# A two-block transformer kernel on one core: the last tiles before two inner norms by halves of the tokens, and the slabs behind each norm split early into memory that is no longer read

## The chip, the core and the metric

The kernel runs on one core of one Trainium2 chip. A core has TensorE (PE, with its weight loads listed as PEld), VectorE (DVE), ScalarE (ACT), GpSimd (POOL) and SyncE (SP), which here only starts transfers. Each engine works through its own list of instructions in order and waits at semaphores for the others. The metric is the device time of one execution in microseconds (us); lower is better.

## What is computed

Two transformer blocks, one behind the other, on 512 tokens of 1024 features, in float32. What matters here is cut out of them:

```python
# first block
mod = silu(c) @ w_ada + b_ada                  # six vectors: sh1, sc1, g1, sh2, sc2, g2
...
mix = concatenate([att, pool], -1) @ w_out
x = x + g1 * mix
h2 = rmsnorm(x, norm2_g) * (1.0 + sc2) + sh2   # "norm 1" below
x = x + g2 * conv_gated_ffn(h2, w_up, conv_w, conv_b, w_down)
# second block
h = rmsnorm_2(x, g_pre_mix) * (1.0 + sc1) + sh1   # "norm 2" below
proj = h @ w_in            # qa ka va qb kb vb, qi (heads i0..i3), ki, wi, two gates
...
def rmsnorm(x, g): return x * rsqrt(mean(x * x, -1) + EPS) * g
```

A norm needs the sum over all 1024 features, so it can't start for a token before the last tile of the product ahead of it is added to `x` for that token.

## The kernel before

The features lie on the 128 partitions, the tokens along the free axis: a *tile* m (0 to 7) is 128 features by 512 tokens, and one bank of PSUM holds one. Each float32 operand is split into a high and a low part (`HH`/`HL`, `WH`/`WL`), and a product is three matmuls per 128 input features: high by high, high by low, low by high. A tile of eight input tiles is so 24 matmuls, one of six input tiles 18.

Weights come as *slabs* of 256 columns (two tiles). SP loads slab i into `RAW[i % 2]` once slab i-2 is split; ACT copies it to `WH[i % 2]` (line 994) once PE has spent slab i-2, and POOL subtracts into `WL[i % 2]` (line 1916). Slabs 5 to 8 are `("out", 0..3)`, 9 and 10 `("gate", 0)` and `("val", 0)`, 39 to 42 `("down", 2, 0..3)`, 43 `ki` (which also holds `wi`), 44 `i01`, 45 `vb0`, 46 `i23`. Between the slabs SP loads the chunks of the modulation matrix (`ada`, 512 KB each, into `ZF`): chunk n+2 once VectorE has taken chunk n (lines 1495 and 1498). A plan (`ada_plan`) fixes at which point of the program each chunk is taken: `("1", s)` is step s of the first attention, `("2", p)` the slab p of the output product, and `sums` says where PE turns the finished vector (line 563).

Around norm `st` (1 or 2) the order was: for each tile m, VectorE adds the product to `x` (lines 1618 and 1664), ACT squares it (998) and multiplies it by its gain (1151), VectorE adds up the squares (1458). Then `norm_two` sums over the partitions with a matrix of ones, ACT takes logarithm and exponential (1013, 1015), VectorE refines the root in four instructions (1442 to 1450, `newton`), multiplies the eight tiles (1478), ACT adds the shift into `HH` (1022), VectorE forms `HL` (1483), and PE's `first_slab` starts. `first_slab` goes over the high parts of its two tiles first and then over the low ones.

Behind norm 2 come the products `ki`, `wi`, `i0` and then steps s of the indexer: scores of head pair c at even steps, a `piece` (half a product) of `i1`, `vb0`, `vb1`, `i2`, `i3`, `bq0`, `bk0` at the steps of `T_I`. `i` products leave out the first 128 tokens (384 columns). Before the scores of step 0, VectorE, POOL and ACT rotate and split `i0`.

Of the kernel before, what the change touches and what calls it, by code (L numbers as in the profile page):

```python
# [13 lines left out]
T = 512  # L14
D = 1024
# [170 lines left out]


# [132 lines left out]
def ada_plan():  # L320
# [22 lines left out]
class Kernel:  # L343


    def __init__(self, nc, ctx, a):
# [95 lines left out]
    def wbuf(self, of, i):  # L442
        nk, nn, _ = self.slabs[self.names[i]]
        return of[:, i % 2, 0:nk * nn].rearrange("p (k n) -> p k n", k=nk)
# [12 lines left out]
T_I = {"i1": 0, "vb0": 2, "vb1": 4, "i2": 6, "i3": 11, "bq0": 16, "bk0": 18}  # L457
# [25 lines left out]
def pe_program(pe, k):  # L483
# [18 lines left out]
    def slab(name, j=7):  # L502
# [3 lines left out]
        return k.wbuf(k.WH, i), k.wbuf(k.WL, i)  # L506
# [19 lines left out]
    def first_slab(name, keys, st):  # L526
# [13 lines left out]
        spend(name, keys[1])  # L540

# [169 lines left out]
    for m in range(4, 8):  # L711
        mix(m, 0, 8)
        if m % 2:
            for p in (m // 2 - 2, m // 2):
                for j in k.sums["2", p]:
                    ada_sum(j)
    norm_two(1)


    def up1(i):  # L720
        c0, n = UP1[i]
        for p in range(c0, c0 + n, 2):
            for g in ("gate", "val"):
                if (g, p) == ("gate", 0):
                    first_slab((g, p), ((g, 0), (g, 1)), 1)
                else:
# [6 lines left out]
    def down(what, i, n):  # L733
# [3 lines left out]
        for p in range(4):  # L737
# [3 lines left out]
            for j in k.sums.get((what, i, p), ()):  # L741
                ada_sum(j)

    up1(0), up1(1), down("down", 0, 8), up1(2), down("down", 1, 8), down("down", 2, 6)
    norm_two(2)


    first_slab("ki", ("ki", "wi"), 2)
    B.deal(main=range(4), s=range(4, 8))

# [13 lines left out]
    piece("i0", 0)  # L764
    piece("i0", 1)
# [5 lines left out]
    for s in range(STEPS_I):  # L771
# [12 lines left out]
        for x, t0 in T_I.items():  # L784
            if 0 <= s - t0 < 2:
# [186 lines left out]
def act_program(act, k):  # L972
# [44 lines left out]
    def shifted(st, shift):  # L1017

        for j in range(8):
            act.wait_ge(v_h["prod", st, j])  # L1020
            act.wait_ge(v_ada["mod", shift])
            e.activation(k.HH[:, j, :], k.slot(j), ACT.Identity, bias=k.MOD[:, shift, j:j + 1]).then_inc(*hh.hit((st, j)))
# [124 lines left out]
    def gain(st, j, ready):  # L1147
        act.wait_ge(ready)
        act.wait_ge(v_ada["gain", st])
        row = {1: 0, 2: 0}[st]  # L1150
        e.activation(k.slot(j), k.XT[:, j, :], ACT.Copy, scale=k.GS[:, row, j:j + 1]).then_inc(*sq.hit(("gain", st, j)))

    for m in range(8):
        if m == 0:
            for q in range(4):
                weights(q)
        elif m in (4, 6):
            weights()
        square_two(1, m, k.XT[:, m, :], v_post["x1", m])
        gain(1, m, v_post["x1", m])  # L1160
    root(("norm", 1), norm_full[1, 7], 1.0 / D, k.RB[:, :])
# [1055 lines left out]
```

## Time and profile before

| | |
|---|---|
| Time, three runs | 1565.91, 1566.36 and 1566.45 us (median 1566.36) |
| The profiled execution | 1566.11 us |
| Its span, first to last instruction | 1564.1 us |
| PE busy | 1411.2 us (90%) |
| VectorE, ScalarE, GpSimd busy | 827.2, 624.4, 705.3 us (53%, 40%, 45%) |
| Chain that ended last, by engine | PE 69%, DVE 15%, ACT 7%, POOL 5%, DMA 2% |
| Mean granted TensorE clock | 0.956 of full speed |

PE is the engine whose work bounds the kernel, so time is lost mainly where PE is idle, and where its clock is at the lower level after that. A row of a timeline gives start, length, engine, line, operation, output and inputs, shape and count, and in brackets the idle time of the engine ahead of it and what ended it.

### The profile page before, as it was taken

What the parts mean: (1) busy time and instruction counts of PE and PEld (TensorE: products, weight loads), DVE (VectorE), ACT (ScalarE), POOL (GpSimd) and SP (SyncE); (2) the same over time, 40 slices, a digit from 0 to 9 for tenths busy, and PEclk for the clock granted to TensorE, in tenths of its full rate; (3) what the DMA queues carried; (4) which work ended last, traced back from release to release, by engine and by line L of the source; (5) the groups of instructions that cost most, each with busy time, mean ns of one, the idle gap of its engine ahead of it and who ended that gap; (6) DMA issues with size and microseconds to landing.
All of it is one profiled execution on the core that took longest, in us unless ns stands there. A gap on an engine that the chain in (4) does not pass through costs nothing.

```text
span 1564.1 us, 16757 instructions
## 1 busy us (share of the span) xinstructions
PE 1411.2 (90%) x6633; PEld 1140.2 (73%) x6633; DVE 827.2 (53%) x1210; ACT 624.4 (40%) x1018; POOL 705.3 (45%) x328
## 2 busy tenths in 40 slices
PE   4679897899999999858999999999878999999995
PEld 2558775688878888657787777788755888888884
DVE  5686525766673563536789975542248321312125
ACT  3345533434341432424466654454334431413231
POOL 1155533455654464234233453335544664646442
PEclk8799998999999999979999999999989999999997
DMA  8424216265656564311122221112221333232311
GB/s 289 139 69 129 82 53 213 70 200 177 198 168 211 175 188 143 101 54 54 54 72 64 77 59 54 54 55 81 81 81 37 98 108 99 90 108 81 108 54 54
DMA packets 143870, 167.49 MB, mean 107 GB/s; under 512 B 14256, under 2 KB 129584, under 8 KB 143792
## 3 DMA queue, kind: packets, MB, share of 16 engines
q1 hardware_dynamic: 143792, 166.42, 34.4%
q8 instruction: 52, 0.85, 0.2%
q14 instruction: 26, 0.21, 0.0%
HBM read 164.31 MB, written 2.10 MB: 106 GB/s over the span
## 4 chain that ended last, share of the span: by engine, by line
PE 69%; DVE 15%; ACT 7%; POOL 5%; DMA 2%; issue 2%; SPq 0%; ACTq 0%; DVEq 0%
PE B L495 66%; POOL WL L1916 4%; ACT WH L994 2%; DVE ZF L1498 1%; DVE SC L1798 1%; DVE SC L1565 1%; DVE ZF L1769 1%; DVE ZF L1854 1%; PE B L563 1%; DVE XT L1856 1%; PE B L661 1%; DVE SC L1447 1%; PE B L839 1%; DVE M L1767 1%; DVE SC L1657 1%
## 5 line engine op out<-in xcount | busy, mean ns | idle before, releaser
L1916 POOL TENSOR_TENSOR WL<-RAW,WH 128x512 fp32r<-128x512 f32 (+2 forms) x175 | 519.4, 2974 | 577.9 <-ACT WH L994 577.8
L495 PE MATMUL B<-HH,WH 128*128 128x512 f32 (+1 forms) x1088 | 442.7, 407 | 47.2 <-POOL WL L1916 23.5
L495 PE MATMUL B<-HH,WL 128*128 128x512 f32 (+1 forms) x1088 | 432.6, 398 | 0.0
L495 PE MATMUL B<-HL,WH 128*128 128x512 f32 (+1 forms) x1088 | 417.8, 393 | 0.0
L495 PE MATMUL B<-ZR,WH 128*128 128x512 f32 x1184 | 367.2, 391 | 6.4 <-POOL ZR L1923 5.0
L994 ACT ACTIVATE WH<-RAW 128x512 fp32r<-128x512 f32 (+2 forms) x175 | 211.7, 1225 | 215.8 <-PE B L495 160.0
L495 PEld LDWEIGHTS B<-HH,WH 128*128 128x128 f32 x1088 | 211.3, 194 | 100.2 <-issue 49.1
L495 PEld LDWEIGHTS B<-ZR,WH 128*128 128x128 f32 x1184 | 223.2, 189 | 53.9 <-POOL ZR L1923 5.4
L495 PEld LDWEIGHTS B<-HH,WL 128*128 128x128 f32 x1088 | 211.0, 194 | 44.3
L495 PEld LDWEIGHTS B<-HL,WH 128*128 128x128 f32 x1088 | 208.5, 192 | 39.0 <-issue 0.5
L495 PE MATMUL B<-ZR,WL 128*128 128x512 f32 x592 | 231.1, 390 | 0.0
L495 PE MATMUL B<-ZR 128*128 128x256 f32 (+4 forms) x904 | 126.7, 328 | 29.6 <-POOL ZR L1923 11.0
L1923 POOL TENSOR_TENSOR ZR<-SC,ZR 128x512 fp32r<-128x512 f32 (+1 forms) x72 | 95.2, 1323 | 117.4 <-ACT ZR L1390 52.8
L495 PEld LDWEIGHTS B<-ZR 128*128 128x128 f32 (+1 forms) x904 | 98.6, 190 | 58.2 <-issue 22.8
L495 PEld LDWEIGHTS B<-ZR,WL 128*128 128x128 f32 x592 | 111.8, 189 | 23.5
L1874 DVE TENSOR_TENSOR SC<-SC 128x512 f32<-128x512 f32 x32 | 56.5, 1766 | 109.8 <-ACT SC L1385 109.8
L1498 DVE SCALAR_TENSOR_TENSOR ZF<-ZF,CA 128x1024 f32<-128x1024 f32 x68 | 96.3, 1417 | 8.1 <-DMA ZF<-in_w_ada 4.9
L1639 DVE SCALAR_TENSOR_TENSOR SC<-B,VT,SC 128x511 f32<-128x511 f32 x44 | 32.9, 747 | 81.4 <-ACT SC L1171 81.4
L1885 DVE TENSOR_TENSOR ZF<-B,ZF 128x512 f32<-128x512 f32 x24 | 16.6, 692 | 101.1 <-PE B L495 101.1
L1321 ACT ACTIVATE ZR<-B 128x128 fp32r<-128x128 f32 (+3 forms) x64 | 28.0, 437 | 101.5 <-PE B L839 101.3
L1458 DVE TENSOR_TENSOR SC<-SC 128x512 f32<-128x512 f32 x24 | 31.7, 1319 | 54.0 <-ACT SC L998 54.0
L1786 DVE TENSOR_TENSOR ZR<-B,ZR 128x128 fp32r<-128x128 f32 (+3 forms) x64 | 31.3, 488 | 51.6 <-ACT ZR L1321 51.3
(188 smaller groups left out, 1343.5 us busy)
## 6 DMA issues: line engine op xcount, KB each, us to landing
ZF<-in_w_ada SPq DMA_DIRECT2D x86, 512.0 KB, 4.3
RAW<-in_w_ff SPq DMA_DIRECT2D x32, 1024.0 KB, 5.3
RAW<-in_w_up SPq DMA_DIRECT2D x22, 1024.0 KB, 8.3
RAW<-in_w_in SPq DMA_DIRECT2D x16, 1024.0 KB, 5.2
RAW<-in_w_in SPq DMA_DIRECT2D x19, 512.0 KB, 5.2
RAW<-in_w_down SPq DMA_DIRECT2D x8, 1024.0 KB, 7.6
G<-in_w_ada SPq DMA_DIRECT2D x10, 512.0 KB, 8.4
RAW<-in_w_out SPq DMA_DIRECT2D x4, 1024.0 KB, 5.0
```

The lines of the kernel that those rows point to most:

```text
L495: return e.matmul(out, l, r, start=start, stop=stop)
L563: t = e.transpose(b[:, 128 * i:128 * i + 128], k.ACC[j % 2][:, 512 * half + 128 * i:512 * half + 128 * i + 128], k.IDN)
L994: e.activation(k.WH[:, i % 2, at], k.RAW[:, i % 2, at], ACT.Copy).then_inc(*w.hit((i, q)))
L1321: e.activation(k.PT2[:, u % 2, 0, KEYS[blk], 128 * (blk % 2):128 * (blk % 2) + 128], B["t2", u][:, 0:128 * (blk + 1)].rearrange("p (j n) - ...
L1458: e.tensor_tensor(k.slot(8), k.slot(8), k.slot(9), ALU.add).then_inc(*acc.hit((st, j)))
L1498: e.scalar_tensor_tensor(out=dst, in0=src, scalar=c, in1=dst, op0=ALU.mult, op1=ALU.add).then_inc(*ada.hit((j, kt)))
L1639: e.scalar_tensor_tensor(out=s[:, 1:T], in0=b[:, 0:T - 1], scalar=k.VT[:, 128 + c:129 + c], in1=s[:, 1:T], op0=ALU.mult, op1=ALU.add).then ...
L1786: e.tensor_tensor(lo, B["t2", u][:, 0:128 * (blk + 1)].rearrange("p (j n) -> p j n", j=blk + 1), hi.bitcast(F32), ALU.subtract).then_inc(* ...
L1874: e.tensor_tensor(k.xg(ch), k.xg(ch), k.xg(ch), ALU.mult).then_inc(*ffn.hit(("sq", ch)))
L1885: e.tensor_tensor(y, b[:, :], y, ALU.add).then_inc(*post.hit(("yadd", i, m)))
L1916: e.tensor_tensor(k.WL[:, i % 2, at], k.RAW[:, i % 2, at], k.WH[:, i % 2, at].bitcast(F32), ALU.subtract).then_inc(*w.hit((i, 3 if q is No ...
L1923: e.tensor_tensor(dst, src, hi.bitcast(F32), ALU.subtract).then_inc(*sig.hit(key))
```

## The change

The tiles 4 to 7 ahead of norms 1 and 2 are computed in two passes, first for tokens 0 to 255 and then for tokens 256 to 511 (`TILES`, `last_tiles`). The norm of the first half is made while PE works on the second pass (`norm_half`, called after four input tiles of tile 4 of the second pass). The matmuls behind the norm are ordered so that four output tiles of two slabs are done by halves (`first_slabs`): `gate 0, gate 1, val 0, val 1` behind norm 1 and `ki, wi, i0, i1` behind norm 2. `i0` and `i1` are now computed for all 512 tokens. The two slabs that these read are split into parts of `ZR` that nothing reads any more (`away`), so they don't wait for a slab to be spent. Slabs around the norms are split in quarters of 512 columns (`quarters`). The plan moves the eight chunks of vector 3 out of the output product and into steps 31 to 38 of the attention, and SP queues the chunks two slabs later. `vb0` moves from steps 2 and 3 to ahead of step 0, and four small copies on ACT move behind the steps of the indexer.

```diff
-        many = {"1": p % 2 == 0 and p < 32, "2": (3, 3, 2, 0)[p % 4], "gate": 2, "val": 2, "down": 2 - point[1]}[g]
+        many = {"1": p % 2 == 0 if p < 31 else 1, "2": 0, "gate": 2, "val": 2, "down": 2 - point[1]}[g]
...
+        self.away = {("gate", 0): 8192, ("val", 0): 12288, "ki": 8192, "i01": 12288}
...
-T_I = {"i1": 0, "vb0": 2, "vb1": 4, "i2": 6, "i3": 11, "bq0": 16, "bk0": 18}
+T_I = {"i1": -2, "vb0": 2, "vb1": 4, "i2": 6, "i3": 11, "bq0": 16, "bk0": 18}
...
+    def first_slabs(names, keys, st, norm):
...
+        high(0, 0)
+        norm()
+        high(0, 1), high(0, 2), high(0, 3)
+        low(0, 0), low(0, 1), low(0, 2), low(0, 3)
+        high(1, 0), high(1, 1), low(1, 0), low(1, 1)
+        spend(names[0], keys[1])
+        high(1, 2), high(1, 3), low(1, 2), low(1, 3)
...
+    def norm_half(st, half):
+
+        b, at = B.take(pe, "main", ("norm", st, half)), HALF[half]
+        pe.wait_ge(acc[st, 6, half])
+        mm(b[:, at], ONES[:, :], k.slot(8)[:, at], True, False)
+        pe.wait_ge(sq[st, 7, half])
+        mm(b[:, at], ONES[:, :], k.slot(9)[:, at], False, True).then_inc(*norm_full.hit((st, 7, half)))
+
+    def last_tiles(tile, norm):
+
+        for half in range(2):
+            for m in range(4, 8):
+                if (m, half) == (4, 1):
+                    tile(m, half, 0, 4)
+                    norm()
+                    tile(m, half, 4, None)
+                else:
+                    tile(m, half, 0, None)
...
+    def norm_by_halves(st, shift, ready, after, between):
+
+
+        for m, half in TILES:
+            between(m, half)
+            square_half(st, m, half, k.XT[:, m, :], ready[(*after, m, half)])
+            if half == 1:
+                shifted(st, shift, 0, (2 * m - 8, 2 * m - 7))
+            if m == 7:
+                at = HALF[half]
+                root(("norm", st, half), norm_full[st, 7, half], 1.0 / D, k.RB[:, at], at)
+            gain(st, m, half)
+        between(8, None)
+        shifted(st, shift, 1)
...
+    def between1(m, half):
+        if (m, half) in ((0, None), (4, 0), (6, 0), (7, 0)):
+            quarters()
...
+    def between2(m, half):
+        if (m, half) in ((2, None), (4, 0), (6, 0)):
+            quarters()
+        if (m, half) in ((4, 1), (5, 1)):
+            quarters(2 * m - 8, 2 * m - 6)
...
+        for m, half in TILES:
+            tile(m, half)
+            add_half(st, m, half)
+            if (m, half) == (7, 0):
+                root(0)
+            if half == 1 and m < 7:
+                products(st, 0, range((0, 3, 6)[m - 4], (3, 6, 8)[m - 4]))
+        low(st, shift, 0, range(5))
+        root(1)
+        low(st, shift, 0, range(5, 8))
+        products(st, 1)
+        low(st, shift, 1)
...
-        point = ("2", k.names[i][1]) if k.names[i][0] == "out" else k.names[i]
-        for n in k.chunks.get(point, ()):
+        for n in k.chunks.get(k.names[i - 2], ()):
             ada(n + 2)
```

SP's queue from the load of `("out", 2)` on, before (`ZF` is a chunk of the modulation matrix, `RAW` a slab, of which `out` takes three transfers):

```order
L2095 DMA RAW<-in_w_out 64x4x256 [waits pool_w]
L2095 DMA RAW<-in_w_out 64x4x256
L2095 DMA RAW<-in_w_out 128x4x256
L2095 DMA ZF<-in_w_ada 128x1024 [waits dve_ada] x3
L2095 DMA RAW<-in_w_out 64x4x256 [waits pool_w]
L2095 DMA RAW<-in_w_out 64x4x256
L2095 DMA RAW<-in_w_out 128x4x256
L2095 DMA ZF<-in_w_ada 128x1024 [waits dve_ada] x3
L2095 DMA RAW<-in_w_up 128x8x256 [waits pool_w]
L2095 DMA ZF<-in_w_ada 128x1024 [waits dve_ada] x2
```

and in the changed kernel, where the first row stands in the steps of the attention:

```order
L2264 DMA ZF<-in_w_ada 128x1024 [waits dve_ada] x8
L2264 DMA RAW<-in_w_out 64x4x256 [waits pool_w]
L2264 DMA RAW<-in_w_out 64x4x256
L2264 DMA RAW<-in_w_out 128x4x256
L2264 DMA RAW<-in_w_out 64x4x256 [waits pool_w]
L2264 DMA RAW<-in_w_out 64x4x256
L2264 DMA RAW<-in_w_out 128x4x256
L2264 DMA RAW<-in_w_up 128x8x256 [waits pool_w] x5
L2264 DMA ZF<-in_w_ada 128x1024 [waits dve_ada] x2
```

Eight chunks stand ahead of `("out", 2)` that stood behind it and behind `("out", 3)`; between the last slabs of the output product there is none.

ScalarE's list from the split of slab 8 to the last square of the output product, before:

```order
L994 ACTIVATE WH<-RAW 128x2048 [waits pe_proj,in_w0]
L998 ACTIVATE SC<-XT 128x512 [waits dve_post,dve_acc]
L1151 ACTIVATE SC<-XT,GS 128x512
L998 ACTIVATE SC<-XT 128x512 [waits dve_post,dve_acc]
L1151 ACTIVATE SC<-XT,GS 128x512
L994 ACTIVATE WH<-RAW 128x2048 [waits pe_proj,in_w1]
L998 ACTIVATE SC<-XT 128x512 [waits dve_post,dve_acc]
L1151 ACTIVATE SC<-XT,GS 128x512
```

and now, for the first pass (line 1091 is the copy of a slab, 1118 the square, 1277 the gain):

```order
L1118 ACTIVATE SC<-XT 128x256 [waits dve_acc,dve_post]
L1277 ACTIVATE SC<-XT,GS 128x256
L1091 ACTIVATE ZR<-RAW 128x512 [waits pe_weigh,in_w1]
L1091 ACTIVATE ZR<-RAW 128x512 x3
L1118 ACTIVATE SC<-XT 128x256 [waits dve_acc,dve_post]
L1277 ACTIVATE SC<-XT,GS 128x256
L1091 ACTIVATE ZR<-RAW 128x512 [waits in_w0]
L1091 ACTIVATE ZR<-RAW 128x512 x3
L1118 ACTIVATE SC<-XT 128x256 [waits dve_acc,dve_post]
L1123 ACTIVATE RB<-B,EPSC 128x256 [waits pe_norm]
```

The copies of slabs 9 and 10 now stand ahead of the squares of tiles 6 and 7 of the first pass, and the second of them waits for a transfer.

## Rows read from the trace of the kernel before

**Rows 1.** Stretches: busy of PE, PEld, DVE, ACT, POOL; granted clock; DMA share, GB/s

```profile
226.00:316.00 90.00, 73.32 (x299) 58.28 (x297) 54.20 (x61) 36.17 (x47) 35.15 (x11) 0.89 0.43 132
316.00:586.00 270.00, 268.17 (x1200) 220.75 (x1200) 166.73 (x173) 98.01 (x101) 149.07 (x44) 1.00 0.60 187
632.00:730.00 98.00, 72.72 (x323) 58.65 (x321) 50.62 (x60) 34.05 (x52) 36.25 (x14) 0.90 0.27 75
```

**Rows 2.** Chain that ended last, 236 to 262 us: start, length, what

```profile
237.90 3.55 DMA ZF<-in_w_ada
...
241.47 1.29 DVE ZF L1498
...
244.46 6.31 DMA RAW<-in_w_out
...
252.78 5.09 POOL WL L1916
```

**Rows 3.** Timeline of PE around norm 1

```profile
258.00 0.77 PE L495 MATMUL B<-HH,WH 128*128 128x512 f32 x1 [10.67 <-POOL WL L1916]
...
271.83 1.03 PE L563 MATMUL B<-CST,ZF 128*128 128x128 f32 x8
...
279.87 0.77 PE L495 MATMUL B<-HH,WH 128*128 128x512 f32 x1 [5.19 <-ACT HH L1022]
...
289.42 3.79 PE L495 MATMUL B<-HL,WH 128*128 128x512 f32 x16
```

**Rows 4.** Timeline of PE around norm 2 and up to the indexer

```profile
653.92 1.10 PE L495 MATMUL B<-SC,ONES 128*128 128x512 f32 x2 [1.16 <-DVE SC L1458]
...
661.52 0.76 PE L495 MATMUL B<-HH,WH 128*128 128x512 f32 x1 [5.19 <-ACT HH L1022]
...
682.91 0.66 PE L495 MATMUL B<-HH,WH 128*128 128x384 f32 x1 [7.73 <-POOL WL L1916]
...
689.18 0.49 PE L769 MATMUL B<-CST,SC 128*128 128x128 f32 x3
...
697.67 1.01 PE L495 MATMUL B<-ZR 64*128 64x256 f32 x6 [8.01 <-POOL ZR L1923]
```

**Rows 5.** Timeline of PE: first and last of six short waits for a slab

```profile
316.07 0.47 PE L495 MATMUL B<-HH,WH 128*128 128x512 f32 x1 [0.89 <-POOL WL L1916]
...
586.28 0.70 PE L495 MATMUL B<-ZR,WH 128*128 128x512 f32 x2 [0.28 <-POOL WL L1916]
```

**Rows 6.** Timeline of PE: matmuls of 256 columns, and the row behind them

```profile
146.59 3.12 PE L495 MATMUL B<-ZR 128*128 128x256 f32 x24
...
149.55 0.40 PE L495 MATMUL B<-HH,WH 128*128 128x512 f32 x1
```

**Rows 7.** Weight loads grouped by line and form: busy, mean ns, idle before

```profile
L495 PEld LDWEIGHTS B<-HH,WH 128*128 128x128 f32 x1088 | 211.3, 194 | 100.2 <-issue 49.1 <-POOL HL L1923 3.6 <-POOL WL L1916 2.2
```

**Rows 8.** Timeline of SP

```profile
203.06 0.33 SPq L2095 DMA_DIRECT2D ZF<-in_w_ada  x1
...
243.15 1.91 SPq L2095 DMA_DIRECT2D RAW<-in_w_out  x3
```

**Rows 9.** Timeline of VectorE and GpSimd where they meet

```profile
235.00 1.18 DVE L1458 TENSOR_TENSOR SC<-SC 128x512 f32<-128x512 f32 x1 [3.19 <-ACT SC L998]
...
231.82 5.50 POOL L1916 TENSOR_TENSOR WL<-RAW,WH 128x512 fp32r<-128x512 f32 x4 [8.26 <-ACT WH L994]
...
691.14 4.76 DVE L1565 TENSOR_TENSOR SC<-SC 128x384 f32<-128x384 f32 x1 [0.65 <-POOL SC L1928]
...
690.99 4.50 POOL L1916 TENSOR_TENSOR WL<-RAW,WH 128x2048 fp32r<-128x2048 f32 x1
```

**Rows 10.** Timeline of VectorE and ScalarE: the products, a short form, small copies

```profile
278.28 4.91 DVE L1478 TENSOR_TENSOR SC<-SC,RB 128x512 f32<-128x512 f32 x8
...
699.11 0.35 DVE L1746 TENSOR_SCALAR ZF<-SC,WI 128x256 f32<-128x256 f32 x1 [3.20 <-ACT SC L1278]
...
665.97 0.71 ACT L1233 ACTIVATE ZR<-CST 128x256 fp32r<-128x256 f32 x2
```

More of the change, by code:

```diff
@@ L184, with tokens, before @@
 UP1 = [(0, 8), (8, 8), (16, 6)]
+HALF = [slice(0, 256), slice(256, 512)]
+TILES = [(m, None) for m in range(4)] + [(m, h) for h in range(2) for m in range(4, 8)]
+def tokens(h):
+    return slice(0, 512) if h is None else HALF[h]
+def before(m, h):
+    return (m - 1, None) if m < 5 else (m - 1, h)
 ORDER2 = ("bq1 bk1 ga0 ga1 ga2 ga3 bq2 bk2 vb2 vb3 ga4 ga5 bq3 bk3 ga6 ga7 aq0 ak0 va0 va1 aq1 ak1 aq2 ak2 va2 va3 "
@@ L710, in pe_program, with out_tile @@
     mix(3, 4, 8)
[L711 to L717, printed above, removed]
+    for j in k.sums["2", 0]:
+        ada_sum(j)
+    def out_tile(m, half, j0, j1):
+        proj(("mix", m, half), ("out", m // 2), 128 * (m % 2), mix_xs, j0, j1, half=half)
+        if half and m % 2 and j1 is None:
+            spend(("out", m // 2), ("mix", m, half))
+    last_tiles(out_tile, lambda: norm_half(1, 0))
     def up1(i):
@@ L736, in down @@
             pe.wait_ge(g_ffn[what, i, j])
-        for p in range(4):
+        last = (what, i) == ("down", 2)
+        for p in range(2 if last else 4):
             proj((what, i, 2 * p), (what, i, p), 0, xs)
@@ L742, in down, with tile @@
                 ada_sum(j)
+        if last:
+            def tile(m, half, j0, j1):
+                proj((what, i, m, half), (what, i, m // 2), 128 * (m % 2), xs, j0, j1, half=half)
+                if half and m % 2 and j1 is None:
+                    spend((what, i, m // 2), (what, i, m, half))
+            last_tiles(tile, lambda: norm_half(2, 0))
     up1(0), up1(1), down("down", 0, 8), up1(2), down("down", 1, 8), down("down", 2, 6)
-    norm_two(2)
-    first_slab("ki", ("ki", "wi"), 2)
-    B.deal(main=range(4), s=range(4, 8))
+    first_slabs(("ki", "i01"), ("ki", "wi", "i0", "i1"), 2, lambda: norm_half(2, 1))
+    mine = [B.of[x] for x in ("ki", "wi", "i0", "i1")]
+    B.deal(main=mine, s=[b for b in range(8) if b not in mine])
     def piece(x, ph):
@@ L784, in pe_program @@
         for x, t0 in T_I.items():
-            if 0 <= s - t0 < 2:
+            if 0 <= s - t0 < 2 and x not in ("i1", "vb0"):
                 piece(x, s - t0)
@@ L1144, in act_program, with gain @@
             weights(SPLIT1[s])
-    def gain(st, j, ready):
-        act.wait_ge(ready)
+    def gain(st, j, half):
         act.wait_ge(v_ada["gain", st])
[L1150 to L1161, printed above, removed]
-    e.preload_act_table_set(SILU)
-    shifted(1, 3)
+        at = tokens(half)
+        e.activation(k.slot(j)[:, at], k.XT[:, j, at], ACT.Copy, scale=k.GS[:, 0, j:j + 1]).then_inc(
+            *sq.hit(("gain", st, j, half)))
+    def between1(m, half):
+        if (m, half) in ((0, None), (4, 0), (6, 0), (7, 0)):
+            quarters()
+        if m == 8:
+            e.preload_act_table_set(SILU)
+    norm_by_halves(1, 3, v_post, ("x1",), between1)
     def tap(g, ch, n):
@@ L1281, in act_program @@
             task(x, s, t0)
+    for dst, src in ((k.IDR, k.IDN), (k.CAR, k.CAUS)):
+        e.activation(dst, src, ACT.Copy)
+    for half in range(2):
+        e.activation(k.PT2[:, half, :, 3, 0:128], k.CST[:, 0:256].rearrange("p (a n) -> p a n", a=2), ACT.Copy, scale=0.0)
     act.wait_ge(score_full["i", 23])
@@ L1864, in dve_program @@
         e.tensor_scalar(k.slot(m), k.XT[:, m, :], k.GS[:, 2, m:m + 1], None, ALU.mult).then_inc(*hl.hit(("gain", 4, m)))
-    normed(4)
+    newton(("norm", 4), 1.0 / D, k.RB[:, :], k.slot(8), k.slot(9))
+    dve.wait_ge(root_["y", ("norm", 4)])
+    for j in range(8):
+        product(4, j)
     low(4, 9)
@@ L1991, in pool_program @@
             low(k.HL[:, g, :], k.MEAN[g], k.HH[:, g, :], a_mix["pool", g], mix, ("pool", g))
[L1994 to L1997 removed]
+    for i in range(5):
+        quarters()
     def up1(i):
@@ L2012, in pool_program @@
     up1(2)
-    for p in range(8):
+    for p in range(4):
         weights()
+    for p in range(4):
+        quarters()
     def task(x, s, t0):
```

218 lines of the change are left out of this document (135 added, 83 removed).

## The prediction, written before the changed kernel was run

> **What bounds the kernel now.** I read the busy shares first: PE is busy 90% of the span, so I looked for the stretches in which it is not. The view by stretches shows three kinds [rows 1]. In the feed-forward part (316 to 586 us) PE is busy 268.17 of 270 us at full clock; there is almost nothing to win. From 226 to 316 us it is busy 73.32 of 90, from 632 to 730 us 72.72 of 98, and in both the granted clock is 0.89 and 0.90, so busy time is lost too. These are the two norms. The waits of PE in them, read from its timeline, give the terms of the sum.
>
> At norm 1 PE stands twice [rows 3]: 10.67 us for a slab, and 5.19 us for the norm itself. After each it runs at the lower clock level: the 48 matmuls from 258.00 to 271.83 took 13.83 us where the pitch at the upper level, (3.79 - 0.39)/15 = 0.227 us [rows 3], makes 10.9; the 32 from 279.87 to 289.42 took 9.55 where it makes 7.3. So norm 1 costs 10.67 + 5.19 + 2.9 + 2.3 = 21.1 us. The chain says why the slab was late [rows 2]: SP could load it only after a modulation chunk had landed (3.55 us) and VectorE had taken it; then the slab took 6.31, and GpSimd 5.09 for its low part.
>
> At norm 2 the waits are 1.16, 5.19, 7.73 (slab `i01`, split behind the rotation of `ki`) and 8.01 (the rotated `i0`, ahead of the first scores) [rows 4], together 22.1; two smaller ones of about 1.0 lie beside them. The lower clock: behind 661.52 as at norm 1, 2.3; from 682.91 to 689.18 24 matmuls of 384 columns took 6.27 us where 24 x 0.227 x 384/512 = 4.1 is due, 2.2; behind 697.67 some 1.5 (estimated as a share of these, from six score matmuls that took 1.01). Sum 22.1 + 1.0 + 6.0 = 29.1 us.
>
> **The change part by part.**
>
> *The waits removed.* With two passes, PE has the second pass (at norm 1 four tiles of 3 us) in front of it while the first half's norm is made, and behind it 64 + 32 half matmuls on the first half of the tokens while the second half's norm is made. All the waits above have work laid over them. Gain before costs: 21.1 + 29.1 = 50.2.
>
> *Halves cost PE.* 24 matmuls of 256 columns went from 146.59 to 149.55, a pitch of 0.123 to 0.124 [rows 6]; two make 0.248 against 0.227, 0.021 more for each former matmul. Norm 1: 4 tiles x 24 and 4 x 24, 192 x 0.021 = 4.0. Norm 2: 4 x 18 and 4 x 24, 168 x 0.021 = 3.5. `i0` and `i1` for 512 instead of 384 tokens: 48 x 0.227/4 = 2.7. Together 10.2. The Trainium skill, "TensorE: Matmul & The Clock Gate", section "Back-to-back issue gap", gives 262 cycles at 256 columns, 109 ns; by it two halves would cost no more than a whole and the sum would be 7.5 us better. The row decides for 0.124, since it is the same stream of weight load and matmul.
>
> *New waits at norm 1.* (a) Slab 7, `("out", 2)`, is now loaded after eight chunks. SP issues one at 203.06 [rows 8]; a chunk's round is issue 0.33, landing 3.55, VectorE 1.29 [rows 2, 8], 5.2 us for two buffers, so one per 2.6; the eighth is taken at about 203.9 + 8 x 2.6 = 224.7. The three transfers take 250.77 - 243.15 = 7.6 [rows 2, 8], a copy of a quarter 0.55, four quarters in GpSimd about 1.3 each [rows 9]: ready at 238 to 239.5. PE is at this tile at about 237 and needs the third and fourth quarter first: 2.3 us. (b) Slab 8 queues behind it in GpSimd, four more quarters and a few additions of VectorE between them: ready at 247, PE there at 245, less what it has to do with the third quarter: 1.9. (c) Slab 10 can be loaded only when slab 8 is split; 5.3 us of landing (the page's median for a feed-forward slab) and 2.2 of copies stand ahead of the square of tile 7, first half, at 255.5; PE asks for it at 254.4: 1.1. (d) The last tiles of the first half's `HH` come after the last square: 1.4. (e) Lower clock behind one of these 1.0, a collision at the end of the attention 0.5, since chunks now lie between VectorE's last steps there. Sum 8.2.
>
> *The lock.* While GpSimd split (four quarters took 5.50 instead of 4 x 1.27), VectorE's sum took 1.18 instead of 0.69, and the 384-column sum took 4.76, nearly the length of the one GpSimd instruction (4.50) that began just ahead of it [rows 9]. So VectorE instructions with two inputs in SBUF and GpSimd exclude one another, one instruction at a time, and here a stall is at most one quarter, 1.3 us. The Trainium skill, "SBUF — State Buffer", section "Who interferes with whom", says the same and speaks against this change: roots, sums of squares and products all have two such inputs and now run during dense splits.
>
> *New waits at norm 2.* The second pass there is only 4 x 18 x 0.124 = 8.9 us. In it VectorE has for each tile an addition, a sum, and three products of 256 columns; products of 512 take 4.91/8 = 0.61, a short form 0.35 [rows 10], so about 2.2 us with ScalarE's square between, against PE's 2.23. Slab 44 is split in the same 8.9 us; counting the lock for the root, two sums and two products, the last `HH` of the first half comes some 5.3 us after PE wants it. Slab 42 gives 0.6. Then the first scores: VectorE turns `wi` before it finishes `i0`, and PE can transpose `wi` only after `vb0`; from there copy 0.2, sum 0.6, ScalarE 0.5, GpSimd 1.0: 2.6 us idle. Lower clock behind these two waits 2.5. Sum 11.0.
>
> *Smaller parts.* Slabs of the feed-forward part are split one slab earlier, and their loads stand ahead of the chunks; the six waits between 0.89 and 0.28 [rows 5] sum to 2.9 and go. The four small copies (two took 0.71 [rows 10], all four about 1.2) stood beside idle PE and now stand ahead of the masks that PE waits for at the end of the indexer: +1.2. The eight chunks in the attention cost nothing but (e): VectorE idles there.
>
> Sum: 50.2 - 10.2 - 8.2 - 11.0 + 2.9 - 1.2 = 22.5 us. From the profiled execution, 1566.11, which lies 0.25 below the median of the three runs, that is 1543.6, on the median 1543.9; I take 1543.5. A difference of 0.2% (3 us) is about what can be told from none.
>
> **The rivals.**
>
> *The new waits are mostly hidden.* If slab 7 lands in time and the chains of halves keep pace, (a) to (e), the 5.3 and the 0.6 and the clock go: up to 16.6 more, 1527; half of it, the middle of the case, 1535. For: my times of (a) and (c) hang on landing times that vary. Against: the order on each engine leaves GpSimd no gap.
>
> *The lock bites harder.* If each root, sum and product of the first half waits for a whole quarter, 8 quarters of 1.3 us lie on the chain at each norm where I count 1.4 and about 3: about 8 more at norm 1, 4 to 6 more at norm 2 with the clock, 1555. For: 4.76 for a sum of 0.55. Against: an instruction in flight is a quarter now, and the second pass of norm 1 lasts 12 us.
>
> *Slower: weight loads bound the halves.* A weight load lasts 194 ns [rows 7]. If behind the slabs each matmul of 256 columns took that, the 2 x (192 + 168) = 720 half matmuls would cost 0.07 more each, 50 us: 1594. It decides from a pitch of 0.124 + 22.5/720 = 0.155 on. Against: the 24 in a row at 0.124 also had a load each.
>
> *The gain doesn't arrive:* norms hidden, but the stage behind is set by VectorE, and the time stays. For: the chain gives it 15%. Against: what VectorE does behind norm 2 starts later by the same time, so it moves along.
>
> **How the numbers follow.** Chances: forecast (1538 to 1550) 0.50; mostly hidden 0.20; the lock 0.17; no gain 0.05; slower by weight loads 0.04; slower for another cause 0.04. The range goes from 1531 to 1555, which leaves out the far end of the hidden case and the last three. Faster 0.88, same 0.04, slower 0.08.
>
> **What would show it.** In the profile after: no wait of PE over 3 us for a slab at norm 1, and a wait of about 2 at its first half tile; matmuls of 256 columns at a pitch of 0.124; the split of slab 10 ending ahead of the square of tile 7; at norm 2 several waits for ACT's `HH` in the first half tile behind the second pass; one wait of 2 to 3 us for GpSimd ahead of the first scores; the masks last at the end of the indexer. Granted clock in both stretches above 0.93. I am wrong if slab 7 comes so late that PE stands over 5 us, if the squares queue behind a slab for longer, or if the half matmuls run at another pitch.

## The result

The changed kernel takes 1568.9 us (median of 15 runs, 1565.6 to 1572.5) where the kernel before took 1565.7 (15 runs, 1563.2 to 1568.0): a ratio of 1.0023, 95% interval 1.0015 to 1.0031. It is slower by 0.2%, where 1543.5 us, a gain of 22.5 us, was forecast. The profiled execution has a span of 1568.6 us.

The view by stretches of the changed kernel answers to [rows 1] (columns: stretch, length, busy us of PE, PEld, VectorE, ScalarE and GpSimd with counts, granted clock of TensorE, DMA share, GB/s):

```profile
226.00:316.00 90.00, 84.81 (x548) 77.42 (x547) 50.38 (x86) 43.01 (x79) 39.99 (x24) 0.98 0.46 136
316.00:586.00 270.00, 252.25 (x1083) 207.85 (x1083) 172.92 (x160) 87.86 (x94) 133.68 (x40) 0.95 0.52 174
632.00:730.00 98.00, 90.13 (x566) 80.11 (x565) 56.18 (x93) 43.48 (x84) 45.07 (x28) 0.95 0.30 85
```

Both norms did what they should: PE is busy 84.8 of 90 us where it was 73.3, and 90.1 of 98 where it was 72.7, and the granted clock rose from 0.89 and 0.90 to 0.98 and 0.95. The loss is in the middle row, in the feed-forward part, of which the prediction said that "there is almost nothing to win". There PE was busy 268.17 us at full clock, and is now busy 252.25 at 0.95. The cause must lie in PE's waits there.

To give each stretch its price I took marks on PE's timeline that stand in both kernels: the last turning of the first attention's sums, the first and the last sum of a modulation vector in the feed-forward part (of seven), and the first scores of the second attention. A *sum* of a modulation vector is the set of eight short matmuls (line 563, now 647) by which PE turns the vector once VectorE has taken its last chunk. Kernel before:

```profile
219.50 0.60 PE L682 MATMUL B<-CST,RB 128*128 128x128 f32 x4
...
337.96 1.04 PE L563 MATMUL B<-CST,ZF 128*128 128x128 f32 x8
...
627.20 1.04 PE L563 MATMUL B<-CST,ZF 128*128 128x128 f32 x8
...
752.63 1.74 PE L495 MATMUL B<-ZR 64*128 64x256 f32 x8 [2.31 <-DVE ZF L1749]
```

Changed kernel, with the five of the seven sums that now wait:

```profile
220.65 0.60 PE L766 MATMUL B<-CST,RB 128*128 128x128 f32 x4
...
330.65 1.94 PE L647 MATMUL B<-CST,ZF 128*128 128x128 f32 x8 [3.56 <-DVE ZF L1663]
...
381.65 1.94 PE L647 MATMUL B<-CST,ZF 128*128 128x128 f32 x8 [3.55 <-DVE ZF L1663]
...
431.12 1.07 PE L647 MATMUL B<-CST,ZF 128*128 128x128 f32 x8 [3.55 <-DVE ZF L1663]
...
480.90 1.94 PE L647 MATMUL B<-CST,ZF 128*128 128x128 f32 x8 [3.55 <-DVE ZF L1663]
...
576.32 1.94 PE L647 MATMUL B<-CST,ZF 128*128 128x128 f32 x8 [3.55 <-DVE ZF L1663]
...
642.67 1.04 PE L647 MATMUL B<-CST,ZF 128*128 128x128 f32 x8
...
757.04 1.74 PE L527 MATMUL B<-ZR 64*128 64x256 f32 x8 [3.31 <-ACT ZR L1413]
```

| stretch | before | changed | difference |
|---|---|---|---|
| norm 1, up to where PE asks for the first sum | 118.5 | 106.4 | -12.0 |
| that wait, and from the first to the last sum | 289.2 | 315.6 | +26.3 |
| norm 2 and the indexer | 125.4 | 114.4 | -11.1 |
| the rest to the end of the span | 811.5 | 811.6 | 0 |

With 1.2 us more ahead of the first mark (220.65 against 219.50) that is the 4.5 us by which the spans differ (1564.1 and 1568.6).

The price of the middle row: five waits of 3.55 us are 17.8 us, and behind each the clock is at its lower level for a while. From 330.65 the 8 short and the next 10 long matmuls took 6.0 us until the pitch was 0.227 us again, where 3.1 is due (0.85 for the eight, ten times 0.227): 2.9 lost. Read in the same way it is 1.4 behind the wait at 381.65 (only three long matmuls were slow), 1.7 at 431.12, 2.9 at 480.90 and 2.9 at 576.32, together 11.7. That makes 29.4 us. (The expectations below have 12.9 for the 11.7: they count 2.8 at 381.65 as well.) Against it stand the short waits for slabs that are gone, 2.0 us in this stretch (the sixth, of 0.89, lies in the row above), and the lower clock behind them.

What PE waits for is VectorE's last modulation chunk. Why VectorE is late shows in the timelines of ScalarE and VectorE ahead of the first of these sums. In the feed-forward part ScalarE takes each finished tile out of PSUM (line 1171, now 1294; the *tap*), VectorE adds the other two terms of the convolution (1639 and 1642, now 1801 and 1804), and for a `val` tile it then multiplies by the gate (1657, now 1819). Kernel before:

```profile
321.84 0.78 ACT L1171 ACTIVATE SC<-B,VT 128x512 f32<-128x512 f32 x1 [0.84 <-PE B L495]
...
324.22 2.01 DVE L1657 TENSOR_TENSOR SC<-SC 128x512 f32<-128x512 f32 x1
...
330.27 3.51 DVE L1498 SCALAR_TENSOR_TENSOR ZF<-ZF,CA 128x1024 f32<-128x1024 f32 x2
```

Changed kernel:

```profile
316.31 1.92 ACT L1091 ACTIVATE WH<-RAW 128x2048 fp32r<-128x2048 f32 x1 [3.16 <-PE B L527]
318.14 0.76 ACT L1294 ACTIVATE SC<-B,VT 128x512 f32<-128x512 f32 x1
...
318.93 0.75 DVE L1801 SCALAR_TENSOR_TENSOR SC<-B,VT,SC 128x511 f32<-128x511 f32 x1 [3.87 <-ACT SC L1294]
...
320.50 2.96 DVE L1819 TENSOR_TENSOR SC<-SC 128x512 f32<-128x512 f32 x1
...
327.01 3.49 DVE L1663 SCALAR_TENSOR_TENSOR ZF<-ZF,CA 128x1024 f32<-128x1024 f32 x2
```

ScalarE's copy of a slab (L1091) stands ahead of the taps (L1294) of two tiles. Now that each slab is copied one place earlier, the copy needs the buffer that PE is still reading, so ScalarE stands until PE has done both tiles of the pair, and only then taps the first. VectorE gets that tile one tile (24 matmuls, 5.45 us) and one copy (1.9) later than before; the chunks stand behind it. Before, VectorE began these two chunks at 330.27 and PE asked at 337.96; now at 327.01 against 327.10. The two chunks take 3.5 us, and that is the wait. VectorE's product is longer too (2.96 us against 2.01, and 0.69 where nothing holds it), and while it was hidden before, it now stands in the chain: the second tap, at 324.03, waits for it. Over the stretch from 316 to 645 us the waits of ScalarE for PE at this line say the same, before (first) and changed (columns: engine and line, waited for: us in total, times, longest):

```profile
ACT WH L994 <- PE B L495: 23.0, 3, 9.0
```

```profile
ACT WH L1091 <- PE B L527: 124.5, 17, 16.0
```

Not all of that is new delay: in e2 below, which has the same order on ScalarE and no wait of PE, it is 74.6 us. The rest is ScalarE standing while PE stands.

### The profile page after: what moved, and what is told of

It is laid out like the page before. It is cut to its first block, busy times and chain, and to the rows that moved or that the text cites. A ratio compares the mean times of both kernels' runs of the same rounds, so it can differ in the third digit from the quotient of the medians.

```text
span 1568.6 us, 17651 instructions
## 1 busy us (share of the span) xinstructions
PE 1427.8 (91%) x7001; PEld 1169.8 (75%) x7001; DVE 852.9 (54%) x1264; ACT 629.7 (40%) x1079; POOL 708.7 (45%) x353
## 4 chain that ended last, share of the span: by engine, by line
PE 71%; DVE 16%; ACT 6%; DMA 3%; issue 2%; POOL 2%; SPq 0%; ACTq 0%; DVEq 0%
PE B L527 68%; DVE ZF L1663 2%; ACT WH L1091 1%; POOL WL L2079 1%; PE B L647 1%; DVE SC L1957 1%; DMA ZF<-in_w_ada 1%; DVE SC L1819 1%; DVE ZF L1928 1%; DVE ZF L2013 1%; DVE XT L2015 1%; PE B L745 1%; PE B L934 1%; DVE M L1926 1%; DVE SC L1574 1%
## 5 line engine op out<-in xcount | busy, mean ns | idle before, releaser
L2079 POOL TENSOR_TENSOR WL<-RAW,WH 128x512 fp32r<-128x512 f32 (+1 forms) x184 | 501.2, 2733 | 595.8 <-ACT WH L1091 595.8
L527 PE MATMUL B<-HH,WH 128*128 128x512 f32 (+2 forms) x1040 | 419.5, 403 | 20.2 <-ACT HH L1133 7.1
L527 PE MATMUL B<-HH,WL 128*128 128x512 f32 (+2 forms) x1040 | 410.1, 394 | 0.0
L527 PE MATMUL B<-HL,WH 128*128 128x512 f32 (+2 forms) x1040 | 403.1, 392 | 0.0
L527 PE MATMUL B<-ZR,WH 128*128 128x512 f32 (+1 forms) x1264 | 373.5, 379 | 6.7 <-POOL ZR L2091 5.0
L1091 ACT ACTIVATE WH<-RAW 128x512 fp32r<-128x512 f32 (+1 forms) x184 | 205.2, 1137 | 263.2 <-PE B L527 248.9
L527 PE MATMUL B<-ZR,WL 128*128 128x512 f32 (+1 forms) x632 | 238.9, 378 | 0.0
L1663 DVE SCALAR_TENSOR_TENSOR ZF<-ZF,CA 128x1024 f32<-128x1024 f32 x68 | 112.7, 1658 | 13.0 <-DMA ZF<-in_w_ada 10.0
L2036 DVE TENSOR_TENSOR SC<-SC 128x512 f32<-128x512 f32 x32 | 56.5, 1766 | 109.8 <-ACT SC L1511 109.8
L647 PE MATMUL B<-CST,ZF 128*128 128x128 f32 x88 | 17.8, 370 | 44.9 <-DVE ZF L1663 41.3
```

The lines of the kernel that those rows point to most:

```text
L527: return e.matmul(out, l, r, start=start, stop=stop)
L647: t = e.transpose(b[:, 128 * i:128 * i + 128], k.ACC[j % 2][:, 512 * half + 128 * i:512 * half + 128 * i + 128], k.IDN)
L1091: e.activation(k.split_of(i)[0][:, at], k.RAW[:, i % 2, at], ACT.Copy).then_inc(*w.hit((i, q)))
L1663: e.scalar_tensor_tensor(out=dst, in0=src, scalar=c, in1=dst, op0=ALU.mult, op1=ALU.add).then_inc(*ada.hit((j, kt)))
L2036: e.tensor_tensor(k.xg(ch), k.xg(ch), k.xg(ch), ALU.mult).then_inc(*ffn.hit(("sq", ch)))
L2079: e.tensor_tensor(lo[:, at], k.RAW[:, i % 2, at], hi[:, at].bitcast(F32), ALU.subtract).then_inc(*w.hit((i, q)))
```

## Experiments

The first four separate three theories: A, the queue of ScalarE (above); B, SyncE's new order of loads, in which chunks stand behind a slab; C, the exclusion of VectorE and GpSimd, since VectorE's product (the expectations call it a sum) took 2.96 us there while GpSimd's split of a slab ran:

```profile
318.31 4.61 POOL L2079 TENSOR_TENSOR WL<-RAW,WH 128x2048 fp32r<-128x2048 f32 x1 [6.06 <-ACT WH L1091]
```

On B the trace of the changed kernel itself says something. Between 290 and 650 us VectorE waited for the transfer of a chunk only twice:

```profile
DVE ZF L1663 <- DMA ZF<-in_w_ada: 3.6, 2, 2.0
```

Both waits (at 508.89 and 520.28 us) lie ahead of the sum at 528.17, which did not wait. So late chunks are not what the five waits come from.

**e1: splits of the feed-forward part one place later again**, on ScalarE and GpSimd, up to slab 40, which is split at the first tile of norm 2 again. The edit, cut down:

```diff
 def up1(i):                     # ScalarE; GpSimd's queue in step
-            if p > 0: weights()
-            else: quarters()
+            if p > 0: weights()
             ... taps of the gate pair
-            weights()
+            if p > 0: weights()
+            else: quarters()
```

> The changed kernel with one thing undone: in the feed-forward part ScalarE (and GpSimd) split each slab one place later in their queues, as in the kernel before (slab 11 in the middle of the first pair, slab 40 at the first tile of norm 2). Theory A (queue): ScalarE's slab copy, now one place earlier, waits for PE to finish both tiles of the pair and holds back the taps of these tiles; VectorE's modulation chunks lie behind them, and PE's sum of the chunks waits 3.55 us five times (17.8 us) and runs at the lower clock level after each (about 2.8 us, 1.6 at one, 12.9 together). Then all five waits go: 1568.9 - 17.8 - 12.9 = 1538 us, up to 2.9 more (1541) if the short waits for slabs in the feed-forward part come back. Theory B (chunks): the chunks are loaded behind slab i for point i-2 and arrive late; then the waits stay, and the time is 1568 or more. Theory C (lock): VectorE's sums are held by GpSimd's splits (2.97 us instead of 0.69); then the waits stay but for 1 to 2 us each, about 1560.

Measured: 1577.3 us (6 runs), ratio 1.0064 (1.0045 to 1.0083). None of the three theories had this: A said 1538, C about 1560, and B, whose "1568 or more" covers the time, said that the waits at the sums would stay. The waits of PE and VectorE from 290 to 650 us (waited for: us in total, times, longest):

```profile
PE B L527 <- POOL WL L2082: 23.4, 16, 3.3
PE B L647 <- DVE ZF L1666: 4.8, 4, 2.2
...
DVE ZF L1666 <- DMA ZF<-in_w_ada: 40.5, 18, 4.1
```

The waits at the sums fell from 17.8 to 4.8, so ScalarE's copy was part of it. But SyncE loads a slab when the slab two ahead is split, and the chunks behind that slab. With the splits later both come later: VectorE waits 40 us for chunks at this line, where it waited 3.6 in the changed kernel, and 11.6 more at the line of a vector's first chunk; PE waits 23 us for slabs. Theory A alone, as a forecast of this run, falls: the place of the splits and the order of the loads are one design in two queues.

**e2: the sums one slab later, all else as changed.** PE turns the vectors, and VectorE takes up the result, one slab later.

```diff
 def ada_plan():
-        sums[point] = due
-        due = []
+        if g in ("1", "2"): sums[point], due = due, []
+        else: sums[point], late, due = late, due, []
```

> The changed kernel, but in the feed-forward part PE sums a finished modulation vector one slab later (10.9 us), with all splits where the change put them. Theory A: VectorE's chunks are late by 3.5 us against a sum that comes 10.9 us too early for them; the five waits go and nothing takes their place, 1538 us. If the lateness of VectorE held up something else of PE as well (PSUM banks, the hidden tiles for the down products), other waits show and the time is over 1545. Theory B (chunks loaded too late): the waits go too, but VectorE shows waits for the chunks' transfers.

Measured: 1539.8 us (4 runs), ratio 0.9827 (0.9813 to 0.9841), 29.1 us below the changed kernel; its waits and the clock behind them were 17.8 + 11.7 = 29.5. Theory A had 1538. The stretch of the feed-forward part:

```profile
316.00:586.00 270.00, 270.00 (x1217) 224.04 (x1216) 208.00 (x175) 96.21 (x101) 142.28 (x44) 1.00 0.57 188
```

PE is never idle. VectorE is as late as in the changed kernel (product 2.96 us, and the two chunks begun at 328.32, later by the 1.3 us by which ScalarE's copy ahead of them is: 317.62 against 316.31); PE only asks later. This is the change with its one large defect mended, and it lies 3.7 us from the forecast.

**e3: the early splits alone, in the kernel before.**

```diff
 def up1(i):                     # ScalarE and GpSimd
             weights()
+            if p == 0: weights()
```

> The kernel before with one thing of the change alone: in the feed-forward part ScalarE and GpSimd split each slab one place earlier in their queues (slab 11 beside slab 10 at the first pair; norm 2 as before). Theory A: the chunks were taken 4.2 us ahead of PE's sum (330.27 + 3.5 against 337.96); they now come one tile and one copy later (5.5 + 1.9), so PE waits about 3.2 us at five or six sums and loses 2.8 us of clock at each: 1566 + 30 = 1596 us, more if slabs, whose loads stand behind chunks in SP here, come late as well. Theory B (order of the chunk loads) has nothing changed here: 1566 us, no wait for chunks.

Measured: 1763.0 us (4 runs), ratio 1.1243. Far more than A's 1596, for the second reason that A gave. Waits of VectorE, PE, ScalarE and SyncE's queue from 290 to 650 us:

```profile
DVE SC L1641 <- ACT SC L1171: 196.9, 32, 12.1
...
PE B L495 <- POOL WL L1918: 63.7, 10, 10.6
PE B L563 <- DVE ZF L1500: 51.6, 4, 13.4
ACT WH L994 <- DMA RAW<-in_w_up: 156.8, 14, 13.1
...
SPq L2099 <- DVE ZF L1500: 269.2, 33, 20.4
```

It is a ring: ScalarE's copy waits for its slab, the slab stands in SyncE's queue behind a chunk, the chunk's buffer waits for VectorE, and VectorE waits for the tap behind the copy (196.9 us, against 81.4 in the kernel before). In the changed kernel the slabs stand ahead of the chunks, and ScalarE waits for no slab at all between 290 and 650 us: the changed order of loads opens this ring. Theory B, that this order does the harm, is refuted.

**e4: the feed-forward slabs in four pieces.** `weights()` becomes `quarters()` on ScalarE and GpSimd, in the same places.

> The changed kernel, with each slab of the feed-forward part split in four pieces on ScalarE and GpSimd, in the same places of the queues. Theory C (lock): VectorE's sum that took 2.97 us behind one GpSimd split of 4.6 us waits at most a quarter (1.3 us): about 1.2 us; the five waits of 3.55 us fall to 1.5 or go, 1545 to 1555 us. Theory A (queue alone): the copies still stand ahead of the taps, and the waits stay at about 3.5 us, 1568 us. If both share the chain, the waits fall to about 1.8 us: 1558 us, since the clock still falls.

Measured: 1556.3 us (4 runs), ratio 0.9932 (0.9917 to 0.9947). It lies just above C's band (1545 to 1555) and near the 1558 for a shared chain. The same product of VectorE, and PE's wait at the first vector's sum:

```profile
323.45 1.84 DVE L1816 TENSOR_TENSOR SC<-SC 128x512 f32<-128x512 f32 x1
...
332.46 1.94 PE L647 MATMUL B<-CST,ZF 128*128 128x128 f32 x8 [2.70 <-DVE ZF L1660]
```

The product takes 1.84 us instead of 2.96 and the five waits are 2.70 instead of 3.55. The exclusion (the Trainium skill, "SBUF — State Buffer", section "Who interferes with whom", states it; the trace agrees) has 0.85 us of each wait, 4.3 in all. The rest of the 12.6 us gained is the clock behind the shorter waits: read as above, the loss is 1.6, 0.1, 0.1, 1.5 and 0.1 us, together 3.3 instead of 11.7. So 12.6 of the 29.4 us go when the slabs are split in pieces, and the other 16.8 stay with the copy where it is. Neither share exists without the moved copy: e5 below splits whole slabs in the old places, and no sum waits.

**e5: splits and loads both as before.** As e1, and SyncE loads the chunks of `names[i]`, not of `names[i - 2]`.

> The changed kernel with two things undone together in the feed-forward part: the splits one place later in the queues of ScalarE and GpSimd, and SyncE's order of loads as in the kernel before (chunks with slab i for its own point, not two slabs later). The runs so far: splits moved back alone 1577, splits moved forward alone in the kernel before 1763. Theory A2 (the two belong together): either order with the other's partner makes loads wait; with both as before the feed-forward part takes what it took (289 us from first to last sum against 312), so PE waits for no chunk: 1566 - 12.0 (norm 1) - 11.1 (norm 2) and up to 2 for the start, 1541 to 1545. Theory D (the halves and the slabs split into dead memory disturb the feed-forward part by themselves): waits stay, 1555 or more.

Measured: 1549.3 us (4 runs), ratio 0.989 (0.987 to 0.991). No sum waits, and from the first to the last sum it takes 288.5 us (289.2 before): the two do belong together (A2), and the halves and the slabs in dead memory (D) do not disturb the feed-forward part by themselves. It is 4 us above the band of A2, because the norm 1 stretch takes 114.7 us (219.59 to 334.34) instead of 106.4. PE's timeline there:

```profile
241.48 0.55 PE L527 MATMUL B<-HH,WH 128*128 128x256 f32 x1 [4.07 <-POOL WL L2082]
...
296.31 0.47 PE L527 MATMUL B<-HH,WH 128*128 128x512 f32 x1 [1.89 <-POOL WL L2082]
...
310.82 0.47 PE L527 MATMUL B<-HH,WH 128*128 128x512 f32 x1 [3.28 <-POOL WL L2082]
```

The wait of 1.89 comes with the late splits: e1 has it too, at the same time. The one of 3.28 hangs on a slab whose load stands behind two chunks; ScalarE waited 2.50 us for it. Why the first is 4.07 where the changed kernel has 2.60 no run isolates: neither edit touches that slab.

**e10: copies behind the taps of their pair.**

```diff
 def up1(i):                     # ScalarE
-            weights()
             ... taps of a pair
+            weights()
```

> The changed kernel with nothing but ScalarE's and GpSimd's order within a pair turned: the taps of a pair first, then the slab copy that stood ahead of them; sums, chunks and loads as in the changed kernel. Theory A (the copy that waits for PE holds back the taps): taps start with their tile, VectorE takes the chunks some 5 us earlier against PE, the five waits of 3.55 us and the low clock behind them go; the splits end 3.5 to 4 us later with a slack of 4.4, so short waits for slabs of up to 1 us may show: 1539 to 1546 us. Theory B (the chunk loads behind the slabs are what is late): they stand later still here, VectorE waits for transfers and PE's waits stay or grow: 1565 to 1580.

Measured: 1581.8 us (4 runs), ratio 1.0098 (1.0075 to 1.0120). My expectation missed again, by the cause of e1: behind the taps of one pair is just ahead of the taps of the next, so this is nearly e1's order, with the same waits (from 290 to 650 us PE 23.8 us for slabs and 5.8 at sums, VectorE 44.0 for chunks). I had reckoned the slack of the splits, 4.4 us, and not that the loads hang on them.

**e7 and e11: norm 2 as in the kernel before, on top of e2** (whole tiles, no slab in dead memory there, `i0` and `i1` for 384 tokens behind the norm).

> The kernel with the sums one slab later (1539.8 us), and norm 2 as in the kernel before: whole tiles, slabs 43 and 44 split after the norm, i0 and i1 for 384 tokens and behind the norm. My terms for norm 2 are a gain of 29.1 less 3.5, 2.7, 11.0 and 1.2: 10.7, and the stretch from the last sum of the feed-forward part to the first scores of the second attention is 11.1 us shorter in the changed kernel: 1550.5 to 1551.5 us, with the waits of 5.2, 7.7 and 8.0 us back. Rival (the stage behind gives it back, or norm 2 profits from the order of the feed-forward part): 1540 to 1545.

> The kernel with norm 2 as before once more, since its six times fell in two groups, 1541.6 to 1542.8 (clock 0.966) and 1551.6 to 1554.3 (clock 0.957), and the profile shows the second. If the groups come from the clock that is granted behind the same waits, the stretch from the last sum to the first scores of the second attention is again 117 us against 105 us, and a profile of the first group shows the same waits with shorter stretches elsewhere.

Measured: e7 1542.8 us (6 runs, in two groups, 1541.6 to 1542.8 and 1551.6 to 1554.3), e11 1542.6 (4 runs). By the medians norm 2 would be worth 3 us. The stretch from the last sum to the first scores says 12: 105.4 us in e2 (622.03 to 727.46), 117.5 in e7, 116.0 in e11. PE's timeline of e11 has the waits of [rows 4] back, these three and the one of 1.16 (now 1.15):

```profile
646.20 0.77 PE L529 MATMUL B<-HH,WH 128*128 128x512 f32 x1 [5.19 <-ACT HH L1135]
...
666.85 0.66 PE L529 MATMUL B<-HH,WH 128*128 128x384 f32 x1 [7.74 <-POOL WL L2089]
...
681.26 1.01 PE L529 MATMUL B<-ZR 64*128 64x256 f32 x6 [8.01 <-POOL ZR L2101]
```

In e7 nothing of it is given back: from the first scores to the end e2 takes 811.0 us and e7, whose profile is of the slower group, 811.2. In e11 this rest takes 805.0, and the part ahead of the last sum is 2.0 us shorter, which hides most of the 10.6. The same 3568 matmuls stand there in all three, and PE is idle for 50.1 to 50.6 us, but it is busy for 760.9 us in e2, 760.7 in e7 and 754.5 in e11, and over the 273 us behind the first scores the granted clock is 1.00 in e11 and 0.98 in e2 and e7: the 6 us are the clock, and the last section has rows of it. So the rival "gives it back" had the time right and the mechanism wrong, and the time of a whole kernel is a poor measure of one stretch here.

**e6: the four small copies in the indexer's steps 12 to 15** (with e2).

> The kernel with the sums one slab later (1539.8 us), and the four small copies of ScalarE (1.2 us) not ahead of the masks but one each in steps 12 to 15 of the indexer. If the copies are what makes PE's wait behind the indexer 3.31 us where it was 2.31: the wait is 2.1 to 2.3 and the time 1538.7. If something else came late there: 1539.8.

Measured: 1533.3 us (4 runs), ratio 0.9787 (0.9769 to 0.9805). PE's wait at the first scores of the second attention is 2.31 again instead of 3.31, as expected, but the time is 5.4 us below the 1538.7 that this gave. By the spans of the two profiles e6 is 6.4 us shorter than e2: 0.7 in the stretch from the last sum to the first scores (104.7 against 105.4), which is all that the edit can claim there, 1.0 ahead of the last sum, where the edit changes nothing, and 4.6 behind the first scores (806.4 against 811.0), where the clock fell for less long.

**e8: slab 7 ahead of the last five chunks** (with e2): SyncE loads it at step 34 of the attention.

> The kernel with the sums one slab later (1539.8 us), and slab 7 loaded at step 34 of the attention, ahead of the last five chunks. If slab 7 is late because it is loaded behind eight chunks (landed at 237.2 with PE there at 238.5): PE's wait of 2.6 us goes and the lower clock behind it (about 1.1), and of the next two waits of 1.23 and 0.45 some part, since slab 8 is split sooner: 1535 us. If instead the chunks, now 2.7 us later, hold up VectorE's additions, or PE's finishing of slab 5 is what the split waits for: 1538 to 1541.

Measured: 1535.5 us (4 runs), ratio 0.9804 (0.9787 to 0.9822). The wait of 2.60 is gone and one of 1.79 is left where 1.23 and 0.45 were, and the last sum comes 4.2 us earlier (617.81 against 622.03); 1535 was expected.

**e9: e2, e6 and e8 together.**

> The changed kernel with the three edits together: sums one slab later, small copies in the steps of the indexer, slab 7 loaded ahead of the last five chunks. If they add: 1539.8 - 6.5 - 4.3 = 1529 us. Of the 6.5 only 1.7 lie ahead of the second attention; the rest are two stretches in which the granted clock happened not to fall. If those fall here as in the kernel without the edit: 1533 to 1534.

Measured: 1531.0 us (4 runs), ratio 0.9773 (0.9754 to 0.9792): 2.3% below the kernel before, the fastest version here. It lies between the 1529 for a plain sum and the 1533 to 1534 for a clock as in the kernel without the edit; from the first scores to the end it takes 804.7 us.

## Why the prediction was wrong

The step that failed is in the part on smaller edits: "Slabs of the feed-forward part are split one slab earlier, and their loads stand ahead of the chunks; the six waits between 0.89 and 0.28 [rows 5] sum to 2.9 and go." The 2.9 itself was right, if anything low: in e2 the five intervals from the first sum to the sixth take 222.2 us instead of 225.2, where 1.8 us of those waits lay. What was missing is a term that stood at nothing. I did not ask what is queued behind the moved copy on ScalarE, and who waits for that. The chain was readable: taps behind the copy, chunks behind the taps, PE's sum behind the chunks, with a slack of 337.96 - 330.27 - 3.5 = 4.2 us against a delay of 7.4. It cost 29.4 us where 0 stood in the sum, and the rival for the other side was a different one, weight loads. None of the signs of being wrong concerned the feed-forward part, since "there is almost nothing to win" there; there was something to lose.

The other terms, by the trace of the changed kernel:

- *Norm 1, removed 21.1, halves 4.0, new waits 8.2: net 8.9 forecast, 12.0 measured.* New waits of PE there:

```profile
241.08 0.55 PE L527 MATMUL B<-HH,WH 128*128 128x256 f32 x1 [2.60 <-POOL WL L2079]
...
250.18 0.35 PE L527 MATMUL B<-HH,WH 128*128 128x256 f32 x1 [1.44 <-POOL WL L2079]
...
259.36 0.70 PE L527 MATMUL B<-SC,ONES 128*128 128x256 f32 x2 [0.68 <-ACT SC L1118]
```

  (a) 2.60 for 2.3; (b) 1.44 and 0.39 for 1.9; (c) 0.68 for 1.1; (d) did not come, for 1.4. The 12.0 also holds the wait of 0.89 that I had counted among the 2.9. Of (e), the collision at the end of the attention cannot be told: the first mark stands 1.2 us later, but over the versions here with the same program up to it, it lies anywhere from about 219.6 to 223.9.
- *Halves.* The pitch of 256 columns is 0.120 us at full clock (246.06 to 246.66 for five), not 0.124: 0.013 for each of 360 matmuls, 4.7 instead of 7.5. The Trainium skill, "TensorE: Matmul & The Clock Gate", section "Back-to-back issue gap", gives 262 cycles for the matmul by itself, by estimate 109 ns at 2.4 GHz; the measured 0.120 us, in a stream with a weight load for each, lies between that and my row of before, and decides. Weight loads did not bound the halves: that rival needed a pitch of 0.155.
- *Norm 2, net 29.1 - 3.5 - 2.7 - 11.0 - 1.2 = 10.7 forecast, 11.1 measured* (12 in e7 and e11). Timeline of PE:

```profile
672.49 0.47 PE L527 MATMUL B<-HH,ZR 128*128 128x256 f32 x2 [0.77 <-POOL ZR L2079]
674.76 0.80 PE L527 MATMUL B<-HH,ZR 128*128 128x256 f32 x2 [1.79 <-ACT HH L1133]
...
676.22 1.19 PE L527 MATMUL B<-HH,ZR 128*128 128x256 f32 x4 [0.67 <-ACT HH L1133]
...
678.19 1.19 PE L527 MATMUL B<-HH,ZR 128*128 128x256 f32 x4 [0.78 <-ACT HH L1133]
...
710.63 1.15 PE L527 MATMUL B<-ZR 64*128 64x256 f32 x12 [2.46 <-POOL ZR L2091]
```

  Waits in the first half tile 4.0 for 5.3, the two for slab 42 0.64 for 0.6, the one ahead of the first scores of the indexer 2.46 for 2.6, the masks 1.0 later for 1.2. That the total is so near is in part luck: the waits of PE in this stretch fell by 14.6 us (28.8 to 14.2) where my terms have 13.4, the halves cost 1.3 less, and so the lower clock must have given back about 1.4 (estimate, as what is left) where I had 6.0 - 2.5 = 3.5. The lock did not bite harder than forecast at the norms. In the feed-forward part, where I had not counted it, it could reach PE once the moved copy had used up the slack: splitting in pieces there takes 12.6 of the 29.4 us away (e4).
- *"The gain doesn't arrive"* came true in the total and not as told: VectorE was not too slow behind the norms, it was made late between them. And that e2, with that mended, lies 3.7 us from the forecast is again a sum of errors on both sides: norm 1 gave 3 us more, and the clock in the second attention, which no term had, moves the total by 5 to 6 us.

## What to carry to other kernels

When an instruction that waits for a buffer is moved up in an engine's queue, the work behind it inherits the wait, also where nothing waits for the moved instruction itself. Follow that work through each engine to whoever asks for it, and set the slack beside the delay. Orders of splits, loads and consumers that wait for each other in a ring have to be moved together, or the consumer has to come later: moving the sums by one slab, with nothing else, brought 29 us. A part that runs at 100% still needs its slack checked when the order in it is touched.

## What the runs showed that I had not expected

The clock behind a wait of 2 to 3 us falls in some executions and not in others, at the same place with the same wait. Behind the wait of 2.31 us at the first scores the eight matmuls took 1.73 us in e7 and 1.06 in e11, which are the same kernel. Two waits of PE in the second attention, in e2 and in e6, whose program there is the same:

```profile
903.85 1.35 PE L529 MATMUL B<-ZR 64*128 64x256 f32 x8 [2.25 <-ACT SC L1440]
...
936.95 1.05 PE L529 MATMUL B<-ZR 64*128 64x256 f32 x8 [2.69 <-ACT SC L1440]
...
967.90 1.06 PE L529 MATMUL B<-ZR 64*128 64x256 f32 x8 [0.52 <-ACT SC L1440]
```

```profile
900.78 1.06 PE L529 MATMUL B<-ZR 64*128 64x256 f32 x8 [2.27 <-ACT SC L1441]
...
932.35 1.06 PE L529 MATMUL B<-ZR 64*128 64x256 f32 x8 [2.69 <-ACT SC L1441]
...
961.75 1.06 PE L529 MATMUL B<-ZR 64*128 64x256 f32 x8 [0.52 <-ACT SC L1441]
```

From the first to the second 33.1 us in one and 31.6 in the other, from the second to the third 31.0 and 29.4. Over the 100 us from the first of these rows the granted clock is 0.97 in e2 and 1.00 in e6. These 3 us, with what lies between the first scores and the first of these rows (176.4 us in e2, 175.1 in e6, 173.8 in e11), make most of the 5 to 6 us between 811 and 805 us for the same rest of the kernel. The five waits of 3.55 us of the changed kernel say the same within one execution: 1.4 us lost behind one, 1.7 behind another and 2.9 behind three. What decides it stays open: the waits are equal, the moment differs. Two versions can so differ by 0.4% in something that neither edit touched, and only stretches between marks tell it apart.
